# Two transformer blocks on one core: expert results added on the chip by products with a slot-to-token matrix, in place of a scatter through HBM

## What is computed

```python
def hier_moe(x, w_group, w_expert, w_gate, w_up, w_down):
    ...
    expert = (g_idx * M_PER_GROUP + e_idx).reshape(-1)
    token = jnp.repeat(jnp.arange(n_tok), M_TOPK)
    order = jnp.argsort(expert)
    tok_sorted = token[order]
    xs = xt[tok_sorted]
    hid = jax.nn.silu(lax.ragged_dot(xs, w_gate, sizes)) * lax.ragged_dot(xs, w_up, sizes)
    ys = lax.ragged_dot(hid, w_down, sizes) * weight.reshape(-1)[order][:, None]
    return jax.ops.segment_sum(ys, tok_sorted, num_segments=n_tok).reshape(b, s, d)
```

## Time and profile before

| what | before |
|---|---|
| median of 3 runs | 2702.6 us (2701.52 to 2705.91) |
| span of the profiled execution, first to last instruction | 2704.4 us |
| PE busy | 2507.2 us, 93% |
| DVE busy | 1077.4 us, 40% |
| ACT busy | 754.9 us, 28% |
| POOL busy | 182.2 us, 7% |
| moved by DMA | 576.56 MB, of it 84 + 84 + 84 + 44 + 44 + 40 + 4 loads of expert weights, 1024 KB each |

### The profile page before, as it was taken

The page is one execution under the profiler, slowest core; times in us unless marked ns, Lnnn a source line. Parts: engine busy times, 40 slices in busy tenths (PEclk is TensorE's granted clock), DMA queues, the critical chain, the costliest instruction groups (busy, mean ns, idle before and its releaser), DMA issues.

```text
span 2704.4 us, 36859 instructions
## 1 busy us (share of the span) xinstructions
PE 2507.2 (93%) x14582; PEld 1852.0 (68%) x14582; DVE 1077.4 (40%) x1628; ACT 754.9 (28%) x1221; POOL 182.2 (7%) x302
## 2 busy tenths in 40 slices
PE   8997999788899979998788899999999999999999
PEld 7675665444576656664454677888888877888887
DVE  4753110100345641110001666656642666556542
ACT  3530000000245410000001353543332454434331
POOL 0001111111000001111111000000000010000000
PEclk9998999999999989999999999999999999999999
DMA  6339999999722189999998422222332312223231
GB/s 172 85 145 382 405 406 409 411 408 406 267 94 79 40 329 405 405 405 411 408 407 334 170 67 90 79 94 94 100 134 93 102 48 95 85 92 103 94 125 55
DMA packets 175401, 576.56 MB, mean 213 GB/s; under 512 B 20560, under 2 KB 104080, under 8 KB 125618
## 3 DMA queue, kind: packets, MB, share of 16 engines
q1 hardware_dynamic: 164722, 558.07, 54.5%
q0 software_dynamic: 10560, 16.81, 1.9%
HBM read 569.56 MB, written 23.07 MB: 219 GB/s over the span
## 4 chain that ended last, share of the span: by engine, by line
PE 68%; SPq 20%; DMA 5%; DVE 3%; issue 3%; ACT 2%; DVEq 0%; POOLq 0%; POOL 0%; ACTq 0%
PE ps L232 16%; PE ps L234 16%; PE ps L233 16%; SPq L1175 13%; SPq L1181 7%; PE ps L1325 6%; PE ps L1343 4%; DMA r_x<-resid 1%; DMA first_ring<-in_moe_w_gate 1%; PE ps L1295 1%; DMA first_weights<-in_moe_w_up 1%; ACT lat_probs L1833 1%; PE ps L1642 1%; PE ps L2330 1%; PE ps L1658 1%
## 5 line engine op out<-in xcount | busy, mean ns | idle before, releaser
L1325 PE MATMUL ps<-first_weights,moe_xsT 128*64 128x256 f32 x2688 | 311.3, 381 | 46.4 <-DMA first_weights<-in_moe_w_up 27.6
L232 PE MATMUL ps<-l_h_hi,l_w_hi 128*128 128x512 f32 x896 | 353.0, 394 | 0.0
L233 PE MATMUL ps<-l_h_lo,l_w_hi 128*128 128x512 f32 x896 | 348.8, 389 | 0.0
L234 PE MATMUL ps<-l_h_hi,l_w_lo 128*128 128x512 f32 x896 | 348.8, 389 | 0.0
L1404 DVE TENSOR_TENSOR moe_hid<-moe_silu,ps 128x256 f32<-128x256 f32 x64 | 27.0, 422 | 783.8 <-PE ps L1325 783.8
L1325 PEld LDWEIGHTS ps<-first_weights,moe_xsT 128*64 128x64 f32 x2688 | 223.9, 137 | 143.6 <-issue 93.7
L2882 DVE TENSOR_TENSOR l_w_lo<-l_raw,l_w_hi 128x2048 fp32r<-128x2048 f32 x76 | 174.1, 2293 | 270.2 <-ACT l_w_hi L2627 270.2
L1377 ACT ACTIVATE moe_ys<-ps 128x512 f32<-128x512 f32 x64 | 38.2, 597 | 678.9 <-PE ps L1343 678.9
L1343 PE MATMUL ps<-first_weights,moe_hidT 128*64 128x512 f32 x672 | 172.1, 658 | 38.3 <-DVE moe_hidT L1406 38.3
L2627 ACT ACTIVATE l_w_hi<-l_raw 128x2048 fp32r<-128x2048 f32 x76 | 145.6, 1918 | 179.4 <-PE ps L234 168.5
L232 PEld LDWEIGHTS ps<-l_h_hi,l_w_hi 128*128 128x128 f32 x896 | 168.3, 188 | 37.4 <-issue 2.9
(11 more groups left out here) (589 smaller groups left out, 4351.3 us busy)
## 6 DMA issues: line engine op xcount, KB each, us to landing
first_weights<-in_moe_w_up SPq DMA_DIRECT2D x84, 1024.0 KB
first_weights<-in_moe_w_down SPq DMA_DIRECT2D x84, 1024.0 KB
first_weights<-in_moe_w_gate SPq DMA_DIRECT2D x84, 1024.0 KB
first_ring<-in_moe_w_up SPq DMA_DIRECT2D x44, 1024.0 KB
first_ring<-in_moe_w_down SPq DMA_DIRECT2D x44, 1024.0 KB
l_raw<-in_ffn_up SPq DMA_DIRECT2D x44, 1024.0 KB, 5.1
first_ring<-in_moe_w_gate SPq DMA_DIRECT2D x40, 1024.0 KB
l_raw<-in_w_in SPq DMA_DIRECT2D x22, 1024.0 KB, 5.2
```

The source lines that it names most:

```text
L232: pe.matmul(out, stationary[0], moving[0], start=first, stop=False)
L233: pe.matmul(out, stationary[0], moving[1], start=False, stop=False)
L234: return pe.matmul(out, stationary[1], moving[0], start=False, stop=last)
L1325: ins = pe.matmul(k.ps[64 * h:64 * h + 64, 2 + m, 0:256], xsT[:, j, :], piece[:, j % 4, 256 * h:256 * h + 256], start=j == 0, stop=j == ND ...
```

## The change

What it does, part by part:

- `r.put`, `r.y_dram`, the scatter, the loads back, the diagonals and `Collect.add` go. `lay` now makes for each slot its token and its weight (`r.slot`); the weight is carried exactly as three bf16 parts, and the second listing product has 250 columns where it had 100.
- For each block POOL copies the column of `r.slot` (`cur`). DVE compares it with a row of token numbers (loaded once per layer by ACT's queue): `place`, 128 slot halves by 512 tokens, ones and zeros. ACT writes the down result times the weight, rounded to float32r (`y_hi`), DVE the rest (`y_lo`).
- PE, behind the down products of the next block, multiplies for each of four token tiles: `place` (64 rows) by `y_hi` and by `y_lo`, for two halves of the columns, four float32r products of 512 columns in a tile, the halves in two row groups of the array and in two banks. Tiles 0 and 2 use banks 4 and 5, tiles 1 and 3 banks 6 and 7.
- DVE adds each tile's two banks to the residual (128x1024). PE's tile t waits for `added` of tile t - 2.
- The last block's results are added after the loop and at the start of the next stage (`add_rest`). The splits of the next stage's first two weight pieces, high on ACT and low on DVE, move from `experts` and from ahead of the norm into the norm's sequence; their loads start earlier.

The diff, cut to its core:

```diff
@@ class Routing
-                ins = pe.matmul(k.ps[SLOTS * h:SLOTS * h + SLOTS, 7, 0:2 * COLS], self.in_slot[:, a, :], self.in_blk[:, a, 2:4, :]...
+                ins = pe.matmul(k.ps[SLOTS * h:SLOTS * h + SLOTS, 7, 0:5 * COLS], self.in_slot[:, a, :], self.in_blk[:, a, 0:5, :]...
...
+        for n in range(3):
+            link(dve.tensor_copy(x.w_part[:, n, :], rest))
+            if n < 2:
+                link(dve.tensor_tensor(x.w_rest[:, :], rest, x.w_part[:, n, :], ALU.subtract))
+                rest = x.w_rest[:, :]
+        for n in range(3):
+            ins = dve.tensor_tensor(part(2 + n), hot, over(x.w_part[:, n]), ALU.mult)
+        ins.then_inc(x.laid, 1)
...
@@ class Collect
+    def combine(self, k, pe, t, bank, fresh):
+        for y in (self.y_hi, self.y_lo):
+            for h in range(2):
+                rows = slice(SLOTS * h, SLOTS * h + SLOTS)
+                ins = pe.matmul(k.ps[:, bank + h, :], self.place[rows, t * P:(t + 1) * P], y[rows, :], start=fresh and y is self.y_hi, stop=y is self.y_lo)
+        return ins
+
+    def add_rest(self, k, pe, t):
+        if t != 2:
+            own(k, pe, t)
+        self.combine(k, pe, t, 2 * t, False).then_inc(self.collected, 1)
@@ experts, SP
-            wait_then_tick(sp, ys_out, n * 16 + (EXPERTS - 1) * 16, tick_sp)
-            wait_then_tick(sp, xsT_kept, n + EXPERTS, tick_sp)
-            cl.load(sp, 0)
...
+            sp.wait_ge(used[WEIGHT_SETS - 1][5], TURNS)
+            cl.load_early(sp, 0, *early(0))
             cl.load_gains(k, sp)
+            cl.load_early(sp, 1, *early(1))
@@ experts, POOL
+                wait_then_tick(pool, ylo_made, b + 1, tick_pool)
+                pool.tensor_copy(cur[:, :, :], r.slot[:, bass.ds(b, 1), :]).then_inc(cur_set, 1)
                 wait_then_tick(pool, rows_turned, b + 2, tick_pool)
                 gather(b + 2)
-                wait_then_tick(pool, ys_out, b * 16, tick_pool)
-                pool.tensor_copy(put[:, :], r.put[:, bass.ds(b, 1)]).then_inc(put_set, 1)
-                wait_then_tick(pool, put_set, b + 1, tick_pool)
-                wait_then_tick(pool, ys_kept, b + 2, tick_pool)
-                pool.indirect_dma_start(out=r.y_dram, ...
@@ experts, PE
+                def combine(t):
+                    if not first:
+                        wait_then_tick(pe, added, b * 4 + (t - 1), tick_pe)
+                        cl.combine(k, pe, t, pair(t), True).then_inc(combined, 1)
+
+                wait_then_tick(pe, ylo_made, b + 1, tick_pe)
                 wait_then_tick(pe, hidT_kept, b + 1, tick_pe)
-                wait_then_tick(pe, ys_kept, b + 1, tick_pe)
...
                 ins.then_inc(used[s][5], 1)
+                for t in range(NT):
+                    combine(t)
@@ experts, ACT
-                act.wait_ge(ys_out, b * 16)
+                act.wait_ge(place_made, b + 1)
                 act.wait_ge(used[s][5], times + 1)
-                act.activation(ys[:, :], k.ps[:, 4, :], ACT.Copy).then_inc(ys_kept, 1)
+                act.activation(cl.y_hi[:, :], y_ps, ACT.Copy, scale=slot_weight).then_inc(yhi_made, 1)
@@ experts, DVE, behind the copy of xsT
+                if not first:
+                    for t in range(NT):
+                        dve.wait_ge(combined, b * 4 + (t - 3))
+                        dve.tensor_tensor(k.resid[:, t, :], k.resid[:, t, :], k.ps[:, pair(t):pair(t) + 2, :]..., ALU.add).then_inc(added, 1)
+                dve.wait_ge(cur_set, b + 1)
+                dve.tensor_scalar(cl.place[:, :], tokens[:, :], slot_token, None, ALU.is_equal).then_inc(place_made, 1)
+                dve.wait_ge(place_made, b + 1)
+                dve.wait_ge(yhi_made, b + 1)
+                dve.scalar_tensor_tensor(cl.y_lo[:, :], y_ps, slot_weight, cl.y_hi[:, :].bitcast(F32), ALU.mult, ALU.subtract).then_inc(ylo_made, 1)
@@ latent_layer, ACT and DVE (second_block alike)
-            act.sem_inc(hi_made, 2)
+            high(0)
             act.wait_ge(cleared, 3)
             cm.root(act, 0)
+            high(1)
...
-            low(1)
             stats(0)
...
+            low(0)
             split_low(0)
             split_low(1)
+            low(1)
```

More of the change, by code:

```diff
@@ L120, in constants @@
     return {"k_cst": c, "k_ropea": angles(inv_a, 8, [0, 64]), "k_ropeb": angles(inv_b, 16, [0, 32, 64, 96]),
+            "k_iota": np.tile(np.arange(SEQ, dtype=np.float32), (P, 1)),
             "k_roper": angles(inv_r, 32, [0, 64]), "k_decay": (ret * HD ** -0.5).astype(np.float32)}
@@ L177, in __init__ @@
         self.ps = nc.alloc_psum_tensor("ps", [P, 8, 512], F32)
[L178 to L179 removed]
+        self.gain_in = nc.alloc_semaphore("gain_in")
     def attention_buffers(self, st):
@@ L540, in load_gains @@
             sp.dma_start(vector[:, :], k.a[name][self.norm, 1:2, :].to_broadcast([P, D])).then_inc(self.gain_in, 16)
-    def diagonals(self, k, act):
-        for t in range(NT):
-            for c in range(TOPK):
-                ins = act.activation(self.diag[:, c, t, :], k.ident, ACT.Copy, scale=self.before.weight[:, c, t:t + 1])
-        ins.then_inc(self.spread, 1)
     def lend(self, st, norm):
@@ L552, in lend @@
         norm.gain, norm.shift, norm.gain_in, norm.gains_at = self.gain, self.shift, self.gain_in, 32 * (self.norm + 1)
-    def add(self, k, pe, t):
-        pe.wait_ge(self.spread, self.norm + 1)
-        pe.wait_ge(self.y_in[t], 16 * (self.norm + 1))
-        for half in range(2):
-            for c in range(TOPK):
-                ins = pe.matmul(k.ps[:, 2 * t + half, :], self.diag[:, c, t, :], self.rows[t][:, c, half * 512:(half + 1) * 512], start=False, stop=c == TOPK - 1)
-        ins.then_inc(self.collected, 1)
+    def combine(self, k, pe, t, bank, fresh):
[8 more added lines that the diff above has]
+        self.combine(k, pe, t, 2 * t, False).then_inc(self.collected, 1)
 def take_turned(k, copy, eng, rt, t, half):
@@ L1311, in later, with body @@
                 return not (isinstance(times, int) and times == 0)
-            def body(s, times, b, ahead=False):
+            def body(s, times, b, ahead=False, first=False):
                 wait_then_tick(pe, xsT_kept, b + 1, tick_pe)
                 wait_then_tick(pe, hid_kept, b + 1, tick_pe)
-                for m in range(2):
+                for m, out in enumerate((gate_ps, up_ps)):
                     for j in range(ND):
@@ L1355, in _ @@
             blocks = n + (EXPERTS - 1)
-            pe.wait_ge(grown, NT)
             wait_then_tick(pe, xsT_kept, blocks + 1, tick_pe)
             wait_then_tick(pe, hidT_kept, blocks, tick_pe)
-            for t in range(2):
-                own(k, pe, t)
-            wait_then_tick(pe, ys_kept, blocks + 1, tick_pe)
+            wait_then_tick(pe, added, blocks * 4 - 3, tick_pe)
+            own(k, pe, 0)
+            wait_then_tick(pe, ylo_made, blocks + 1, tick_pe)
+            cl.combine(k, pe, 0, 0, False)
+            wait_then_tick(pe, added, blocks * 4, tick_pe)
             own(k, pe, 2)
-            own(k, pe, 3)
         @block.scalar
@@ L1392, in _ @@
             dve.sem_inc(hid_kept, 1)
-            dve.sem_inc(ys_kept, 1)
+            dve.sem_inc(ylo_made, 1)
+            dve.sem_inc(added, 4)
             dve.wait_ge(rows_turned, 1)
@@ L2850, in _ @@
             finish(opening, 0, None)
+            high(0, 1)
             deviation(1)
+            act.wait_ge(cl.collected, NT - 1)
             finish(opening, 1, None)
@@ L3108, in _ @@
             finish(opening, 1)
+            low(0, 0)
             split_low(opening, 0)
             split_low(opening, 1)
+            low(0, 1)
             stats(2)
```

171 lines of the change are left out of this document (79 added, 92 removed).

## The result

The change takes **2849.99 us** (median of 4 runs, 2848.71 to 2850.28) where the kernel before takes 2702.28: a ratio of 1.0537, 95% interval 1.0524 to 1.0549. It is slower by 147.7 us, on the side that was forecast, but the 2917 us that were forecast lie 67 us above it.

The account below looks back on a forecast made before the run. PE limits first, DMA later; the added PE phase makes PE the bound throughout. On 2704.4 us: 204 for the blocks, 6.5 ahead, 4 behind, giving 2918.9, or 2917 us against the median; range 2850 to 2988.

Parts of the forecast that it names:

- the phase: Added stretch on PE behind the down products: 3.9 us a block, of which only 1.8 are products.
- two sums in the chain: Tiles 2 and 3 wait for DVE's sums of tiles 0 and 1, 1.22 us each, within the added PE stretch.
- The tile itself: PE's products for one token tile: costed at 0.45 us if pairs run side by side, 0.91 if not.
- the halves pair: The two column halves of a tile run side by side on PE; if not, 0.9 us more a block.
- one fall of 1.70 us in each block: PE's clock dropping from 2.4 to 1.2 GHz every block: upper bound and rival, 2975 us; chance 0.16, shared with unpaired halves.
- the first low stretch: PE's idle stretch before the down products, 0.91 us waiting for `hidT`; 0.44 clock falls a block, 0.74 us.
- The rival "no added falls": The new PE idle time costs no clock, old falls stay: +79.8 us a layer, 2873 us; chance 0.24.
- the lower end of the range: 2850 us: the 2917 forecast less two DVE sums at 0.67 us (66), 2851.
- a swing of the clock: Skill page's pattern, PE stepping through PSUM banks and idling often; unpriced there, cited for the upper end, 2975 us.
- Ahead and behind: Work before and after the expert blocks: +6.5 us (3 to 10) ahead, +4 us (-6 to +14) behind.
- The check that misled: Sign in the later profile's expert blocks: DMA share well under 1, 350 to 370 GB/s, if the forecast is right.

Follow-up runs that it names:

- experiment 1: Kernel before, with PE's wait for the copied result moved ahead of its wait for `hidT`: 2704.12 us, ratio 0.9993.
- experiment 3: Changed kernel, with PE's wait for `y_lo` put back behind its wait for `hidT`: 2865.23 us, ratio 1.0595.
- experiment 2: Kernel before, with one more wait and counter between `hidT` and the down products: 2705.47 us, ratio 1.0003.
- experiment 8: Changed kernel, without the products of `y_lo` and with sums of 512 of the 1024 columns: 2771.70 us, ratio 1.0243.
- experiment 9: Changed kernel split: tiles 2 and 3 moved between next block's gate and up products, DVE's token-number wait moved to the second block: 2739.97 us, ratio 1.0131.
- experiment 10: Changed kernel with the added products split over two places, token-number wait moved later, and products of `y_lo` left out: 2699.23 us, ratio 0.9975.

## Why the prediction was right or wrong

**Right: what bounds the phase.** Forecast 3.9 us with two sums in the chain; measured 3.94 on the timeline, and 4.1 as the difference of the periods (16.95 less 12.87), since the change of form ahead of the first product falls outside the 3.94. The sums take 1.215 us (1.22), and halving them took 1.07 us off a block. Tile 2 waits 0.95 us, within the 0.6 to 1 that was named, tile 3 only 0.40. The tile itself was mis-sized: 0.57 us (a first pair at 0.33, the second at 0.24), not 0.45; it hides in tiles 1 and 2. `place`, `y_hi` and `y_lo` lie beneath the next products, and the halves pair.

**Wrong: the clock.** The step that failed is "From below it adds no fall, from above one fall of 1.70 us in each block; I take as many as the first low stretch has, 0.44 a block". Its lower bound, no added fall, was set too high: past the first block there is no fall at all, neither a new one nor an old one (granted clock 1.00 where about 0.92 was forecast). The moved wait takes the old ones away by itself (experiment 1), the phase nearly all of them (experiment 3). Why an idle stretch brings a fall in one place and not in another stays open; experiments 2, 8 and 9 show that neither its length nor the length of the period decides alone. The 0.44 itself was a little high: the 16 periods of 13.76 us hold six falls, 0.38 a block, and the last of them, 14.79 us, holds none but 1.9 us of waiting for weights. In numbers, for layer 0: forecast 565.8 us between the silus, measured 529.2. The falls in the sum, old ones at 31 x 0.74 and new ones at 30 x 0.74, are 45.1 us too many; the moved wait takes 31 x 0.15 = 4.7; against that stand 30 x 0.2 = 6 for the phase, 5.0 for the token numbers, and about 2.5 for every third period, which is 17.3 us (PE stands still there at the turn of its loop over three blocks; no run tests it). Together -36, which is the difference. The rival "no added falls" kept the old falls and came out at 2873 us, above the result; with them gone too (31 x 0.74 x 2 = 46 us) it would have been 2827. The longer phase (12 us), the wait for the token numbers (10.7) and the loop's turns (5), less the moved wait (9), make up most of the rest. That the time came so near the lower end of the range is luck: 2850 stood for two sums of 0.67 us, and they took 1.215.

The page of the Trainium skill that the forecast named ("TensorE: Matmul & The Clock Gate", "A second HAM failure mode: psum-queue depth-cycling") describes a swing of the clock when PE steps through PSUM banks and often stands idle for a moment between its groups of products. In after the trace doesn't show it: 0.76, 0.95 and 0.40 us of waiting a block, clock 1.00. With 1.53 us before tile 3 there is such a swing, in 37 of 62 blocks. The page names no length of idle time by which the two could have been told apart.

**Wrong by omission.** The move of PE's wait ahead of `hidT_kept` was in the diff and was not costed: 0.15 us a block, and by experiment 1 enough to take all falls of before away. DVE's wait for `tokens_in`, also in the diff, was not costed either: 10.7 us in all. Each would have needed one line, "what is queued behind this wait".

**Ahead and behind.** Forecast +6.5 and +4, measured 7.6 - 3.0 + 7.3 = +11.9. The sum is about right, by luck, since its parts are not. These parts differ from execution to execution: in five other versions that don't touch what stands ahead of the first silu it starts at 239.2 to 241.5 us, so some 2 us of the 7.6 may be no cost of the change. Ahead of layer 0 the forecast had 4 and the turn starts at 233.07 against 226.12. The timeline of after there:

```profile
225.24 2.72 PE L322 MATMUL ps<-win_in_blk,win_in_slot 128*64 128x250 bf16 x16 [4.28 <-DVE win_in_blk L421]
227.89 3.85 PE L204 MATMUL ps<-cst 128*128 128x512 f32 x6
```

PE waits 4.28 us for DVE's weight operations ahead of the second listing, which itself takes 2.72 us, so the run-on products start 7.0 us later (220.92 in the earlier trace rows) and take 3.85 us for 3.39. The steps were those forecast, but the turn starts at 233.07 where they were to reach 230.3: the first listing starts 1.0 us later than in before, DVE's operations take 4.28 us for 3.5, and the run-on products are longer. In layer 0's tail the way from the last down products to the first norm is 10.5 us (780.15 to 790.66) where 11.8 was forecast and 14.9 were before. Behind layer 1 the forecast named the phase and the sum that `second_block` waits for; no run takes those 7.3 us apart.

**The check that misled.** "DMA's share well under 1, at 350 to 370 GB/s": the rate came true (368 and 376), the share didn't, it is 0.96 and 0.98. PE's groups show no wait for a load. The rate is no sure sign either: the split version moves 404 GB/s at a share of 1.01 from 300 to 700 us, and PE waits for nothing but `hidT`. Only waits for a load, as in the last blocks of experiment 10, show that transfers set the pace.

## What to carry to other kernels

Read a wait's place before its length: the same 16 products and four sums cost 147.7 us where PE had to wait for each pair of banks, and 35 us (ratio 1.0131) when other products stood between and one wait of DVE stood later. When PE gets a new stretch of waits, its clock has three cases, not two: falls are added, stay, or go; a kernel change should be costed with the falls of before removed as one end. And an operation that is off the path in steady state can stand first in a queue: list what each new wait holds up in the first iteration as well.

## What was not expected of the hardware

- 0.15 us of idle time made all the difference to the clock in the blocks of before: at 0.76 us ahead of the down products no series was slow, at 0.91 us 11 of 31 were, at 1.06 us 10 of 31 (5.35 us in place of 3.65).
- A phase of 16 products and 1.35 us of waiting, put into each block, took falls away: 5 in 62 periods with the same 0.91 us ahead of the down products.
- Taking work from PE gained nothing: 8 products fewer a block made the plain period 0.46 us shorter and brought 21 falls in 62 blocks; the time was 6 us more, with overlapping intervals.
- The transfers' share of busy time was 0.98 at 376 GB/s in after, and 1.01 at 404 GB/s in the split version, with PE waiting for no weight in either, against 1.02 at 403 to 407 GB/s in the kernel before, where they were the bound of the later blocks.
- The 256 KB of token numbers, asked for while the weights stream, were there 11.5 us later (237.04 to 248.5, by the wait on them).
